# The tokens of the first two experts of each layer: selected on TensorE out of on-chip rows instead of gathered from memory

## The reference

```
def hierarchical_moe(h, w_r1, b_r1, w_r2, b_r2, w_gate, w_up, w_down):
    x2 = h.reshape(-1, d)
    group_prob = jax.nn.softmax((x2 @ w_r1) + b_r1, axis=-1)
    gp, gi = lax.top_k(group_prob, 1)                      # 1 of 4 groups
    fine = ((x2 @ w_r2) + b_r2).reshape(n_tok, 4, 8)
    sel = jnp.einsum('tg,tge->te', jax.nn.one_hot(gi[:, 0], 4), fine)
    ev, ei = lax.top_k(sel, 2)                             # 2 of its 8 experts
    gates = gp * jax.nn.softmax(ev, axis=-1)
    experts = gi * 8 + ei
    ...
    # per expert e, on its tokens: y = (silu(x @ w_gate[e]) * (x @ w_up[e])) @ w_down[e], times the gate, added per token
```

## Time and profile before

| | us |
|---|---|
| median of 3 runs | 1721.79 (1719.36 to 1758.09) |
| profiled execution, its own time | 1725.76 |
| its span, first to last instruction | 1723.9 |
| PE busy in the span | 1655.6 (96%) |
| DVE busy | 746.2 (43%) |
| ACT busy | 327.9 (19%) |
| POOL busy | 77.0 (4%) |
| bytes moved by DMA | 475.29 MB, mean 276 GB/s |

### The profile page before, as it was taken

One profiled execution on the slowest core, in us unless ns is written; L12 is line 12 of the kernel. 1 busy time (PEld: TensorE's weight loads), 2 busy tenths in 40 slices (PEclk: granted clock), 3 DMA queues, 4 the chain that ended last, 5 costly groups with the idle time before them and its releaser, 6 DMA issues.

```text
span 1723.9 us, 24248 instructions
## 1 busy us (share of the span) xinstructions
PE 1655.6 (96%) x10111; PEld 1089.4 (63%) x10111; DVE 746.2 (43%) x1285; ACT 327.9 (19%) x545; POOL 77.0 (4%) x76
## 2 busy tenths in 40 slices
PE   8999998999999999989999999999999999999996
PEld 6876686555555555547787787878655555555553
DVE  4899744333333333334453444444423332333334
ACT  4224621001001000023221222222010101010002
POOL 0030001000000000000000000000100000000000
PEclk9999999999999999999999999999999999999998
DMA  8212138999999999984222122127699999999994
GB/s 298 98 55 92 60 148 332 399 403 401 397 408 405 399 399 405 407 342 147 76 71 98 49 98 98 66 102 317 225 398 404 405 405 410 405 406 399 401 403 198
DMA packets 109553, 475.29 MB, mean 276 GB/s; under 512 B 10752, under 2 KB 23040, under 8 KB 76544
## 3 DMA queue, kind: packets, MB, share of 16 engines
q1 hardware_dynamic: 101120, 455.11, 67.3%
q0 software_dynamic: 5248, 8.40, 1.7%
q10 hardware_dynamic: 3072, 10.18, 1.5%
HBM read 476.27 MB, written 6.29 MB: 280 GB/s over the span
## 4 chain that ended last, share of the span: by engine, by line
PE 85%; DVE 9%; DMA 2%; ACT 2%; issue 1%; SPq 0%; DVEq 0%; ACTq 0%; POOLq 0%
PE psum L921 25%; PE psum L945 13%; PE psum L836 9%; PE psum L837 9%; PE psum L838 9%; PE psum L1032 8%; DVE h L2056 2%; PE psum L912 2%; PE psum L1314 2%; DVE xs L1720 2%; PE psum L930 2%; DMA in_pair<-in_expert_w_up 1%; DVE w_lo L660 1%; PE psum L936 1%; PE psum L1204 1%
## 5 line engine op out<-in xcount | busy, mean ns | idle before, releaser
L2056 DVE TENSOR_TENSOR h<-h,psum 128x512 f32<-128x512 f32 x240 | 154.2, 684 | 248.1 <-PE psum L1032 248.1
L660 DVE TENSOR_TENSOR w_lo<-raw,w_hi 128x2048 fp32r<-128x2048 f32 x46 | 105.4, 2291 | 202.1 <-ACT w_hi L654 202.1
L945 PE MATMUL psum<-raw,hidT 128*64 128x512 f32 x672 | 155.0, 603 | 1.1 <-ACT hidT L1515 1.1
L654 ACT ACTIVATE w_hi<-raw 128x2048 fp32r<-128x2048 f32 x46 | 88.0, 1914 | 335.0 <-PE psum L838 334.9
L836 PE MATMUL psum<-w_hi,uT_hi 128*128 128x512 f32 x352 | 139.7, 397 | 3.6 <-DVE h L2174 1.4
L1533 ACT ACTIVATE y_hi<-psum,rt 128x512 fp32r<-128x512 f32 x62 | 42.6, 688 | 515.9 <-PE psum L1032 368.8
L838 PE MATMUL psum<-w_lo,uT_hi 128*128 128x512 f32 x352 | 137.8, 392 | 0.0
L837 PE MATMUL psum<-w_hi,uT_lo 128*128 128x512 f32 x352 | 137.8, 391 | 0.0
L1032 PE MATMUL psum<-y_hi,to_token 64*128 64x512 f32 (+1 forms) x464 | 107.7, 446 | 20.6 <-DVE h L2056 17.7
L2292 POOL DMA_INDIRECT x_e<-xs_dram,index x64 | 60.5, 946 | 1469.8 <-PE psum L912 787.9
L2035 DVE SCALAR_TENSOR_TENSOR y_lo<-psum,rt,y_hi 128x512 fp32r<-128x512 f32 x66 | 49.2, 748 | 137.5 <-ACT y_hi L1533 137.3
(11 more groups left out here) (252 smaller groups left out, 2509.8 us busy)
## 6 DMA issues: line engine op xcount, KB each, us to landing
raw<-in_expert_w_down SPq DMA_DIRECT2D x84, 1024.0 KB, 23.8
raw<-in_expert_w_up SPq DMA_DIRECT2D x44, 1024.0 KB, 23.6
free_a<-in_expert_w_gate SPq DMA_DIRECT2D x44, 1024.0 KB, 23.5
in_pair<-in_expert_w_up SPq DMA_DIRECT2D x42, 1024.0 KB, 23.7
in_uT<-in_expert_w_up SPq DMA_DIRECT2D x42, 1024.0 KB, 24.2
free_b<-in_expert_w_gate SPq DMA_DIRECT2D x40, 1024.0 KB, 23.4
in_pair<-in_expert_w_down SPq DMA_DIRECT2D x40, 1024.0 KB, 23.8
xs<-in_expert_w_gate SPq DMA_DIRECT2D x40, 1024.0 KB, 23.6
```

Source lines behind the costliest of these rows:

```text
L654: nc.scalar.activation(part(w_hi[half]), half_of(n, half, by_columns), ACT.Copy).then_inc(hi_ok[half], 1)
L660: nc.vector.tensor_tensor(part(w_lo[half]), half_of(n, half, by_columns), part(w_hi[half]).bitcast(F32), ALU.subtract).then_inc(lo_ok[half ...
L945: mm = nc.tensor.matmul(psum[c * FIRST:(c + 1) * FIRST, bank], x[:, j % 2, (j // 2) * FIRST:(j // 2 + 1) * FIRST], w[:, j, c * 512:(c + 1) ...
L2056: ins = V.tensor_tensor(dst, dst, psum[:, SUM_BANKS[half]], ALU.add)
```

## The change

The tokens of experts 0 and 1 of each layer are no longer gathered. DVE makes `oh_direct`, for each of the two experts and each tile a 0/1 matrix of 128 tokens by 64 places; an unchosen token gets the place 4096, which matches none. PE multiplies the tokens in `xs` with it, 8 x 4 matmuls an expert, and has the tokens transposed in bank 0, where the transposes of the gathered rows put them. Expert 0's stand in front of the lists, expert 1's in step 0 between the gate product and "up". The product "slot_gate" moves into step 0 as well. Of the fillers only 8 stay at one place. POOL gathers from expert 2 on. As `xs` is read in step 0, block 8 waits for the tokens of expert 1. `oh_first` gets another place in memory.

```diff
-WARM = (46, 17, 27, 12, 14)
+WARM = (46, 8)
+DIRECT = 2
...
-            return layer * (STEPS // 2) + e // 2 + 1
+            return layer * ((STEPS - DIRECT) // 2) + (e - DIRECT) // 2 + 1
...
                 if n == RING - 1:
                     sp.wait_ge(xs_stored, 16 * (layer + 1))
-                    full_bank("norm", 2 * layer + 1, TILES - 1, 1)
+                    sp.wait_ge(m.xT_psum, STEPS * layer + DIRECT)
...
+                warm(banks.at("table", layer)[0], WARM[1])
+                pe.wait_ge(bank_free[0], banks.before_experts[layer][0])
+                pe.wait_ge(direct_ok, layer + 1)
+                direct_tokens(layer, 0)
                 dst, full = open_bank("table", layer)
-                warm(banks.at("table", layer)[0], WARM[1])
                 pe.wait_ge(placed, 2 * layer + 1)
...
-                for b in range(8):
-                    pe.wait_ge(bank_free[b], banks.before_experts[layer][b])
-                pe.wait_ge(m.gathered[0], 16 * times(layer, 0))
-                transpose_tokens(m, x_e[:, 0], FIRST)
-                warm(2, WARM[4])
...
                     pe.wait_ge(m.xT_ok, past + e + 1)
+                    if not e:
+                        copied(pe, "table", layer)
                     w, ready = weights("gate", e)
                     product(xeT[:, e % 2], w, 2, ready, m.gate_psum)
+                    if not e:
+                        slot_gates()
                     if e:
                         turned(layer, e - 1)
                     sum_tile(e, 0)
-                    if e < STEPS - 1:
+                    if e + 1 < DIRECT:
+                        direct_tokens(layer, e + 1)
+                    elif e < STEPS - 1:
...
+            def direct_tokens(layer, e):
+
+                for j in range(KC):
+                    for q in range(TILES):
+                        mm = nc.tensor.matmul(psum[:, 0, j * FIRST:(j + 1) * FIRST], xs[:, q * DM + j:(q + 1) * DM:KC],
+                                              oh_direct[:, e, q], start=(q == 0), stop=(q == TILES - 1))
+                mm.then_inc(main.xT_psum, 1)
...
+                link(V.tensor_tensor(place_direct, place_direct, pos[:, :, 0:DIRECT].rearrange("p q e -> p e q"), ALU.add))
+                V.tensor_tensor(oh_direct[:].rearrange("p e q t -> p (e q) t"),
+                                slot_no[:, 0:FIRST].unsqueeze(1).broadcast_to([P, DIRECT * TILES, FIRST]),
+                                place_direct.rearrange("p e q -> p (e q)").unsqueeze(2)
+                                .broadcast_to([P, DIRECT * TILES, FIRST]), ALU.is_equal).then_inc(direct_ok, 1)
...
                 copied(dve, "pos", layer)
+                copy_tokens(main, STEPS * layer + 1, xeT[:, 0], FIRST)
                 src, free = bank("table", layer)
...
-                gather(m, 0, 0)
-                gather(m, 1, 1)
+                gather(m, DIRECT, 0)
+                gather(m, DIRECT + 1, 1)
```

More of the change, by code:

```diff
@@ L399, in trunk_kernel @@
         to_token = place("to_token", [P, 2, 2, P], F32R, at=token_at + 2 * (KC + HC) * P)
-        oh_first = place("oh_first", [P, TOPK * TILES, P], F32R, at=token_at)
+        oh_first = place("oh_first", [P, TOPK * TILES, P], F32R, at=shared + 2 * DM)
+        oh_direct = place("oh_direct", [P, DIRECT, TILES, FIRST], at=token_at + 2 * (KC + HC) * P)
         y_hi.append(place("y_hi2", [P, 512], F32R, at=token_at))
@@ L546, in trunk_kernel @@
         gates_ok = sem("gates_ok")
+        direct_ok = sem("direct_ok")
         spill_ok = sem("spill_ok")
@@ L990, in experts, with slot_gates @@
                 mm.then_inc(full, 1)
[L991 to L1000, removed]
-                for b in range(8):
-                    pe.wait_ge(bank_free[b], banks.before_experts[layer][b])
-                pe.wait_ge(m.gathered[0], 16 * times(layer, 0))
-                transpose_tokens(m, x_e[:, 0], FIRST)
-                warm(2, WARM[4])
+                def slot_gates():
+                    dst, full = open_bank("slot_gate", layer)
+                    pe.wait_ge(placed, 2 * layer + 2)
+                    for k in range(TOPK * TILES):
+                        mm = nc.tensor.matmul(dst[:, 0:EXPERTS], oh_first[:, k].bitcast(F32),
+                                              prod[:, k * EXPERTS:(k + 1) * EXPERTS],
+                                              start=(k == 0), stop=(k == TOPK * TILES - 1))
+                    mm.then_inc(full, 1)
                 def weights(kind, e):
@@ L1036, in experts @@
                 for e in range(STEPS):
-                    if e:
+                    if e == 1:
+                        pe.wait_ge(m.silu_ok, past + e)
+                        for b in range(8):
+                            pe.wait_ge(bank_free[b], banks.before_experts[layer][b])
+                    elif e:
                         pe.wait_ge(m.silu_ok, past + e)
@@ L1054, in experts @@
                     sum_tile(e, 2)
+                    if not e:
+                        copied(pe, "slot_gate", layer)
                     w, ready = weights("up", e)
@@ L1903, in route @@
                                           .broadcast_to([P, TILES, EXPERTS]), ALU.mult)
+                dve.wait_ge(chosen, layer + 1)
+                link(V.tensor_scalar(place_direct, both[:, :, 0:DIRECT].rearrange("p q e -> p e q"), -EMPTY, EMPTY,
+                                     ALU.mult, ALU.add))
                 src, free = bank("pos", layer)
                 pos = src[:, 0:TILES * EXPERTS].rearrange("p (q n) -> p q n", q=TILES)
+                link(V.tensor_tensor(place_direct, place_direct, pos[:, :, 0:DIRECT].rearrange("p q e -> p e q"), ALU.add))
[3 more added lines that the diff above has]
+                                .broadcast_to([P, DIRECT * TILES, FIRST]), ALU.is_equal).then_inc(direct_ok, 1)
                 link(V.tensor_tensor(prod.rearrange("p (k q n) -> p k q n", k=TOPK, q=TILES), chosen_all,
@@ L2062, in moe @@
                 route(layer)
-                copy_tokens(m, past + 1, xeT[:, 0], FIRST)
                 dve.wait_ge(gates_ok, layer + 1)
@@ L2316, in _ @@
                 pool.wait_ge(xs_stored, 16 * (layer + 1))
-                gather(m, 0, 0)
-                gather(m, 1, 1)
[L2319 to L2323, removed]
+                gather(m, DIRECT, 0)
+                gather(m, DIRECT + 1, 1)
+                pool.wait_ge(index_ok, 2 * layer + 2)
+                for e in range(EARLY, STEPS):
+                    pool.wait_ge(m.xT_psum, past + e - 1)
+                    gather(m, e, e % 2)
                 pool.wait_ge(spill_ok, layer + 1)
```

1 line of the change is left out of this document (added).

## The result

The change makes the kernel slower: 1768.50 and 1770.88 us against 1718.77, 1719.36 and 1721.79 without the change, ratio 1.0288 (95% interval 1.0271 to 1.0305).

What follows compares the result with a forecast made beforehand. The saturated weight stream (about 400 GB/s), its start and remaining blocks, was taken to set the expert stages. Losses of 4.4 us in layer 0 and 3.65 in layer 1 summed to +8.05, giving 1729.8 us, range 1721 to 1741.

Steps and rivals of the forecast that it cites:

- the spacing: Direct-token matmuls on PE: one record each 0.111 us, 64 records, 7.1 us per expert.
- the far end: Upper bound for the direct-token loads read at stride eight: 0.156 us each, 10.0 us per expert.
- strided weights: Rival, 15%: the direct loads' spacing follows the strided load, +2.9 us per expert, 1741 us in all.
- The rule that spoke against it: Skill page on SBUF reads: each new 16-byte line pays, f32 strides up to 4 are free; here it is 8.
- PE now has no long pause: Expert 0's gate product, layer 0: full clock expected, so 3.45 us instead of 4.29.
- Release of block 8: SP issues block 8 after expert 1's direct tokens: 287.05 us in layer 0, 1233.5 in layer 1.
- The hold: Block 8 waits for expert 1's tokens and moves into the full stream: 5.2 us a layer, net 4.55.
- 4.4 and 3.65: Loss in us at the ends of layers 0 and 1; layer 1's 6.35 less 2.7 of slack.
- the -1 to 0: Total if PE's path decides: -1.1 us in layer 0, its end wait gone, +0.9 in layer 1.
- The waits for weights: PE's idle time for weight DMAs: 0.5 us before, several us after, all in the layers' last steps.
- The stream absorbs the block: Rival, 14%: queues find room for block 8's 2 MB in 460 us; 1721 us (1718 to 1724).
- Clock falls in the starved steps: Rival, 10%: PE's clock falls while waiting for weights in each layer's last steps, 2 to 4 us per layer; 1735 to 1738.

Runs made afterwards that it cites:

- run seven: The kernel before the change, with only the channel order of the normalised rows in xs permuted block-wise; 1719.57 and 1724.13 us.
- run one: The changed kernel with the direct tokens' weights read from xs at neighbouring elements instead of every eighth (wrong channels); 1731.14 to 1736.35 us, ratio 1.0069.
- run five: The changed kernel with xs written channel-block by channel-block, so direct tokens and transposes load contiguously, values correct; 1730.42 to 1736.12 us, ratio 1.0079.
- run four: The changed kernel with load steps of 2 and 4 elements in layer 0, 8 and 1 in layer 1; executed once, no total time given.
- run two: The kernel before the change, with only block 8 made to wait for the tokens of expert 1; 1728.35 to 1733.05 us, ratio 1.006.
- run six: The changed kernel with direct tokens read from h at neighbouring elements and block 8 waiting as before the change; 1723.19 to 1729.1 us, ratio 1.0027.
- run three: The changed kernel with direct tokens read from h at stride eight and block 8 waiting as before the change; 1759.49 to 1765.54 us, ratio 1.0242.
- run nine: The kernel of run five with only expert 0 direct; expert 1 gathered again, block 8 waiting only for expert 0's set; ratio 0.9983.
- run eight: The changed kernel, strided, with one warm filler product behind each four direct matmuls; 1771.75 to 1772.99 us, ratio 1.0299.

## Why the prediction was wrong

**The step that failed** is the spacing: "not below 0.111, which every 128-column load here shows ... I keep 0.111; the far end is 0.111 x 197/141 = 0.156". It measured 0.238 us, above even the far end. So even the rival *strided weights*, which had the right cause, gave 2.9 us per set where it is 8.1 to 8.3, and 1741 us for 1770. The two readings behind it were wrong in an instructive way. The transposes of the earlier trace rows do come at the same spacing from strided and contiguous tiles, but they stream 128 columns behind each load, and at that length the moving side may set the pace. With 64 columns and 64 rows the stride shows in transposes too: those of the gathered rows, eight in 1.11 us, take 0.71 when contiguous (run seven), from one to the next 0.110 us against 0.062. A transpose's strided load of 0.110 can hide behind 128 columns, which come every 0.109 to 0.113 us in either layout; a product's, at 0.238, can't. The reason is argued; that transposes and products pay differently is measured. The trace of before held the strided half of this comparison, not the contiguous one. And the mean durations, 197 against 141 ns, are no measure of cost for loads that overlap the work before them; a ratio of spacings would have been. For the direct loads themselves the rows are 335 ns strided in the changed kernel and 217 contiguous in run one. The 217 mixes in the set that fell to 1.2 GHz; in run five, where all 256 ran at 2.4 GHz, it is 192. That is a ratio of 1.74, where the spacing is in the ratio 2.1:

```profile
L1078 PEld LDWEIGHTS psum<-oh_direct,xs 128*128 128x128 f32 x256 | 61.3, 335 | 1.0 <-issue 1.0
```

```profile
L1078 PEld LDWEIGHTS psum<-oh_direct,xs 128*128 128x128 f32 x256 | 33.6, 217 | 1.0 <-issue 1.0
```

The attention's products were the right row for the form but not for the layout.

**The rule that spoke against it** was set aside on that reading. The Trainium skill's page "SBUF — State Buffer", section "Door 1: The DMA port swizzle", has it that a read at a wide stride pays at each new line. Runs one and four agree that it does (0.112 against 0.238 us); its figure of 4 f32 for a free stride does not hold for these loads, where a step of 4 already costs 0.233 and only a step of 2 is nearly free, 0.118.

**The clock.** "PE now has no long pause" was right, and the conclusion, that the clock stays up, was not: it fell within sets without any pause. Why it fell no run shows; it did in each of the 14 sets at a step of 4 or 8, and in one of 19 contiguous ones. It made the gate product 6.48 us from start to next start instead of 3.45, and the table product with its copy 2.2 instead of 1.3. The sets themselves it left as they were.

**The sum, mended.** Release of block 8 behind the counts in layer 0, forecast at 21.75: the two sets +8.1 and +8.3 over the 7.1 each, the gate product +3.0, the table +0.9, small hand-overs 0.3. That is 20.6, and 21.75 + 20.6 = 42.4, as measured. Layer 1 has the same rows. With 20.6 a layer the forecast of +8 becomes +49; the profiled executions show +45.1, the ratio of all stands for +50.

**What held.** The order of the steps and their lengths otherwise: with contiguous loads every row of layer 0 came within 0.8 us of its place (run one), block 8 the latest. The hold, "out of the idle stretch into the stream", and the sum that it makes: by the same measure of the stages, the repaired kernel (run five) ends layer 0 2.8 us and layer 1 3.4 us later than the profiled execution of before, where the forecast had 4.4 and 3.65; the hold alone (run two) 3.8 and 3.3. By the ratios these kernels are 14 and 10 us slower, not 8. The forecast read its starting point from the profiled execution of before, which was 5 us over its median. Run six shows what that does: without the hold it takes 1724.03 us when profiled, 1.7 under that execution, near the -1 to 0 that the forecast had for this case, but by the medians it is 3.6 over. The hold itself, 10 us, was forecast at 8 to 9. The waits for weights came where they were looked for, at the ends of both layers. *The stream absorbs the block* is refuted by run two. *Clock falls in the starved steps*: it fell, but at the start.

## What to carry to other kernels

Before tokens are taken out of rows on the chip by matmul, look at the layout that the weight load sees: at steps of 4 and 8 f32 each load took twice as long here, and a loop of 64-column matmuls showed it in full. Judge such a load by the spacing of back-to-back loads under few moving columns, not by the mean length of one, and not under a moving side that is as long as the load. And look at what stands in front of the release of a buffer in a saturated weight stream: moving one block of 2 MB out of the idle stretch cost some 5 us a layer (runs two and six), and once the stream waited for that release, 39.8 us of delay in front of it became 39.3 in the total (run five), though PE's own path would by itself have cost nearly as much (run three). Holding the buffer for one expert's tokens instead of two took the kernel from 14 us over before to 2 to 3 under it (run nine). Check afterwards whether PE or the last landing sets the time before shortening PE's path further.

## What the runs showed of the hardware

- From one f32 weight load of 128 x 128 to the next: 0.112, 0.118, 0.233, 0.238 us at steps 1, 2, 4, 8. At half clock the contiguous one takes 0.213, the one of step 8 stays at 0.238. So something other than PE's clock sets the strided load's time; it was the same out of `xs` and out of `h`, and beside 418 and 2 GB/s of transfers.
- Transposes pay less: with 64 rows and 64 columns 0.062 us from one to the next contiguous and 0.110 at step 8 (run seven, before); with 128 columns 0.109 and some 0.111.
- The granted clock fell from 2.4 to 1.2 GHz within sets in which PE was busy without a pause: 1.0 to 5.5 us behind the start of every set at step 4 or 8 (14 sets: the changed kernel, runs three, four and eight), and in contiguous sets of the same instructions in one of 19 (the second of layer 1 in run one, after 2.0 us). It also fell 1.0 and 1.6 us behind the end of a contiguous set in layer 1 of runs nine and six. Fillers among the strided loads did not hold it.
